# Expert weights of a mixture-of-experts layer: odd pieces issued by GpSimd, even pieces by SyncE

## The reference, cut to what matters

```
def hier_moe(h, lp):
    x = h.reshape(Bn * T, D)
    g_logits = x @ lp['router_group_w'] + lp['router_group_b']
    g_star = argmax(g_logits)                       # one group of 4 experts per token
    ...                                             # top 2 experts in the group -> gate
    hid = silu(einsum('nd,edf->nef', x, lp['expert_w1'])) * einsum('nd,edf->nef', x, lp['expert_w3'])
    y = einsum('nef,efd->nd', hid * gate[:, :, None], lp['expert_w2'])
```

## Time and profile before

| what | value |
|---|---|
| median of 3 runs | 2029.57 us (2023.04 to 2037.4) |
| the profiled execution's own time | 2022.37 us |
| its span, first to last instruction | 2020.7 us |
| start of the first item's gather / of its first matmul | 1358.15 / 1372.97 us |
| stages of the four items from the turn of one item to the next | about 157 us each, 1374 to 2003 us |
| PE, DVE, ACT, POOL busy | 81%, 60%, 40%, 14% of the span |

### The profile page before, as it was taken

How to read it: one execution, slowest core, us unless ns; L and a number is a source line. 1 busy time by engine, 2 the same in 40 slices (tenths; PEclk the granted TensorE clock), 3 DMA queues, 4 the chain that set the end, 5 groups by cost and what they waited for, 6 DMA issues and landing times. The chain is left out here.

```text
span 2020.7 us, 25909 instructions
## 1 busy us (share of the span) xinstructions
PE 1639.8 (81%) x8192; PEld 1285.0 (64%) x8192; DVE 1205.8 (60%) x1686; ACT 808.1 (40%) x997; POOL 274.9 (14%) x352
## 2 busy tenths in 40 slices
PE   4899999999789788884502489657999999999998
PEld 3799996555677555553301367555786787787785
DVE  4233323653344445545798653465788788788788
ACT  4222223434255323231100432214676676577575
POOL 1000004342200445422234000010000000000000
PEclk9899999999677799997755689858999999999999
DMA  5744459996343668752000274135998898898897
GB/s 163 218 137 132 137 136 183 163 162 99 73 161 100 140 145 181 154 111 59 0 0 3 85 208 166 44 120 179 336 374 281 324 372 300 306 360 318 296 371 257
DMA packets 325410, 371.74 MB, mean 184 GB/s; under 512 B 193845, under 2 KB 227922, under 8 KB 314850
## 3 DMA queue, kind: packets, MB, share of 16 engines
q1 hardware_dynamic: 309650, 327.71, 53.7%
q0 software_dynamic: 14544, 43.01, 9.6%
q10 hardware_dynamic: 1152, 0.26, 0.1%
HBM read 362.84 MB, written 19.47 MB: 189 GB/s over the span
## 5 line engine op out<-in xcount | busy, mean ns | idle before, releaser
L154 DVE TENSOR_TENSOR w_low<-w_raw,w_high 128x2048 fp32r<-128x2048 f32 x212 | 484.6, 2291 | 159.5 <-ACT w_high L150 158.1
L150 ACT CAST w_high<-w_raw 128x2048 fp32r<-128x2048 f32 x212 | 403.8, 1911 | 234.7 <-PE ex_A L161 126.8
L159 PE MATMUL ex_A<-w_high,ex_XT_high 128*128 128x512 f32 x512 | 209.9, 410 | 0.0
L160 PE MATMUL ex_A<-w_low,ex_XT_high 128*128 128x512 f32 x512 | 207.3, 405 | 0.0
L161 PE MATMUL ex_A<-w_high,ex_XT 128*128 128x512 f32 x512 | 207.1, 404 | 0.0
L159 PE MATMUL proj_acc<-w_in_high,hT_high 128*128 128x296 f32 x448 | 135.1, 302 | 14.9 <-DVE w_in_low L154 14.9
L446 POOL DMA_DIRECT2D cmp_pages<-in_cache_kv_cmp x128 | 87.3, 686 | 384.8 <-issue 384.8
L160 PE MATMUL proj_acc<-w_in_low,hT_high 128*128 128x296 f32 x448 | 135.2, 302 | 0.0
L161 PE MATMUL proj_acc<-w_in_high,hT_low 128*128 128x296 f32 x448 | 134.7, 301 | 0.0
L569 PE MATMUL cmp_zps<-cmp_xT,cmp_w1s 128*128 128x512 f32 (+1 forms) x288 | 119.2, 569 | 10.3 <-DVE cmp_xT L623 6.7
L154 DVE TENSOR_TENSOR w_in_low<-w_in_slot,w_in_high 128x1184 fp32r<-128x1184 f32 x56 | 76.5, 1389 | 81.0 <-ACT w_in_high L150 81.0
(11 more groups left out here) (519 smaller groups left out, 3070.0 us busy)
## 6 DMA issues: line engine op xcount, KB each, us to landing
w_raw<-in_expert_w SPq DMA_DIRECT2D x196, 1024.0 KB, 5.3
w_in_slot<-in_w_in SPq DMA_DIRECT2D x56, 592.0 KB, 5.0
cmp_pages<-in_cache_kv_cmp POOLq DMA_DIRECT2D x128, 128.0 KB, 7.9
cmp_pages<-in_cache_kv_cmp SPq DMA_DIRECT2D x128, 128.0 KB, 6.9
w_raw<-in_w_out SPq DMA_DIRECT2D x16, 1024.0 KB, 6.4
sel_k_rows<-in_cache_kv_sel POOLq DMA_DIRECT2D x64, 128.0 KB, 3.4
sel_k_rows<-in_cache_kv_sel SPq DMA_DIRECT2D x64, 128.0 KB, 3.5
sel_v_rows<-in_cache_kv_sel SPq DMA_DIRECT2D x64, 128.0 KB, 3.8
```

The costliest lines, as they stand in the source:

```text
L150: return copy(high.bitcast(F32R), x)
L154: return dve.tensor_tensor(low.bitcast(F32R), x, high, ALU.subtract)
L159: pe.matmul(out, r(a_high), r(b_high), start=start, stop=False)
L160: pe.matmul(out, r(a_high), r(b_low), start=False, stop=False)
```

## The change

Odd pieces (1, 3, 5, ...) are issued by POOL, even pieces remain with SP. The waits on `w_low` are the same ones. Before each odd piece POOL also waits for its previous pace instruction and runs a new one, a 1x1 tensor_tensor on `pace` that reads `eps` twice. POOL's loop over items now issues odd pieces 5 to 15, then the gather of the next item, then odd pieces 17 to 47, then pieces 1 and 3 of the next item. The first gather still comes ahead of the loop.

```diff
@@ phase_out @@
             stream_load(sp, z)
-            for n in range(RING):
+            for n in range(0, RING, 2):
                 sp.wait_ge(z.low, 4 * NCH - 3 + n)
                 expert_piece(sp, m, io, 0, n)
+
+        @block.gpsimd
+        def _(pool):
+            for n in range(1, RING, 2):
+                pool.wait_ge(z.low, 4 * NCH - 3 + n)
+                expert_piece(pool, m, io, 0, n)
...
 PLACES_AT = 8
+FETCH_AT = PLACES_AT + 9
@@ phase_moe @@
+        def load(eng, w, item, chunks):
+
+            e0 = eng.value_load(m.plan[0:1, bass.ds(item, 1)], min_val=0, max_val=12)
+            for n in chunks:
+                eng.wait_ge(w_low, w * CHUNKS + (n + 1))
+                if n % 2:
+                    eng.wait_ge(paced, w * (CHUNKS // 2) + ((n - RING) // 2 + 1))
+                    eng.tensor_tensor(pace[:], eps[:1], eps[:1], ALU.mult).then_inc(paced, 1)
+                expert_piece(eng, m, io, e0, n)
...
             pool.sem_inc(paused, 1)
+            pool.sem_inc(paced, 1)
...
             fetch(0)
             with pool.Fori(0, count(pool)) as w:
+                load(pool, w, w, range(RING + 1, FETCH_AT, 2))
                 pool.wait_ge(x_made, w * 4 + 4)
                 fetch(w + 1)
+                load(pool, w, w, range(FETCH_AT, CHUNKS, 2))
+                load(pool, w, w + 1, range(CHUNKS + 1, CHUNKS + RING, 2))
 
         @block.sync
         def _(sp):
             sp.sem_inc(w_low, RING)
-
-            def load(w, item, chunks):
-
-                e0 = sp.value_load(m.plan[0:1, bass.ds(item, 1)], min_val=0, max_val=12)
-                for n in chunks:
-                    sp.wait_ge(w_low, w * CHUNKS + (n + 1))
-                    expert_piece(sp, m, io, e0, n)
-
             with sp.Fori(0, count(sp)) as w:
-                load(w, w, range(RING, CHUNKS))
-                load(w, w + 1, range(CHUNKS, CHUNKS + RING))
+                load(sp, w, w, range(RING, CHUNKS, 2))
+                load(sp, w, w + 1, range(CHUNKS, CHUNKS + RING, 2))
```

More of the change, by code:

```diff
@@ L2254, in phase_moe @@
         idx = ctx.enter_context(nc.sbuf_tensor("ex_token", [P, 1], I32))
-        pause, eps = sb("ex_pause", [1, 1]), m.eps
+        pause, pace, eps = sb("ex_pause", [1, 1]), sb("ex_pace", [1, 1]), m.eps
         X = m.proj[:, 0, D:2 * D]
@@ L2267, in phase_moe @@
         id_made, id_ready, x_in, paused = n_("id_made"), n_("id_ready"), n_("x_in"), n_("paused")
+        paced = n_("paced")
         order = ORDER
```

## The result

| kernel | median | runs |
|---|---|---|
| before, on the same chip | 2026.3 us | 2021.97 to 2037.4, 4 runs |
| after | 2118.01 us | 2103.98 to 2121.63, 4 runs |

The ratio is 1.0431, 95% interval 1.0364 to 1.0498: slower by some 90 us, and above the top of the range.

The account below looks back on a forecast made before the run. PE was taken to set the pace, with the DMA engines close behind at 98% busy. All steady terms cost 0 and only the start gained: 2029.57 - 3.4 = 2026.2 us, range 2009 to 2066 us.

Parts of the forecast that it names:

- trigger and landing: Odd pieces on POOL in the steady stretch: 6.1 us from DVE's end to landed, 0.9 us to spare, cost 0.
- The 6.96 us of a turn: Part of one buffer's 11.20 us left for trigger, issue and landing after 4.24 us from ACT's start to DVE's end.
- The trigger, 0.42 us: Time from DVE's end to POOL's issue of an odd piece, read at the gather, against SP's 0.17 us.
- about three times an item: How often DVE runs two low parts back to back; only there would a pace lose 2.29 us, swallowed, cost 0.
- Rival 2: Pace waits behind DVE's low part; if every odd piece met it, +42 us, 2068 us; chance 0.08.
- 2 us of idle time in front: Sign of a slower outcome: pace instructions on POOL preceded by 2 us of idle time.
- The landing, 5.7 us: Landing of a POOL piece: SP's 5.3 us plus POOL's longer issue, 0.75 against 0.37 us.
- shares 0.4 us ... and can lose that much: Contention of two queues: a POOL piece overlaps the next SP piece by 0.4 us, within its 0.9 to spare; cost 0.
- 2.63 us per MB against 2.80: Two queues' throughput at the stage's start against steady demand of one piece per 2.80 us: fits with 6% left.
- The cushions: Steady stretch: 1.5 us to spare in SP's reload, plus 3.9 us that ACT may be late before PE waits.
- Rival 1: POOL's pieces land late and the buffers bind: PE loses 9.9 d - 3.9 four times, middle 2064 us; chance 0.16.
- The start, -3.4 us: Stage start: with fewer pieces beside it, the first gather lands at 1363.9 instead of 1367.25 us, a 3.4 us gain.

## Why the prediction was wrong

The step that failed is "trigger and landing are 0.42 + 5.7 = 6.1 of 6.96: 0.9 us to spare, PE keeps its pace, cost 0". In the medians they took 0.67 + 7.2 = 7.9 us without the pace, and with it 2.2 + 7.5 = 9.7 where the pace was long; PE stood still in the changed kernel, and a turn took 14.70 us instead of 11.20.

- **The bound** was read rightly: PE at the limit and the DMA engines close behind, more to lose than to win. The 6.96 us of a turn were right too: 14.70 - 11.20 = 3.50 us were lost in just this place.
- **The trigger, 0.42 us, failed.** It was read at the gather, behind a short DVE instruction. For a piece it is 0.69 us (low part's end at 1640.65 to the issue at 1641.34) where the pace is short. It is 2.2 us where the pace is long: the first of the two low parts ended at about 1634.66, half of 4.50 after 1632.41, and the issue came at 1636.90. So a POOL piece comes 1.0 us later than SP's even without the pace, not 0.6.
- **"So the pace is through before the next low part" and "about three times an item" failed.** Some 44% of the pace instructions met a low part, about ten an item. The count of back-to-back low parts came from a trace in which loads were spaced evenly; the change itself makes them come in pairs. Rival 2 was dismissed by that count. Its sign, "2 us of idle time in front" of the pace, came in another form: the instruction itself is recorded as 2.08 us long.
- **The landing, 5.7 us, and "shares 0.4 us ... and can lose that much" failed.** POOL's queue alone gave 6.1, so the queue's own price was nearly right. What was missing is that late odd loads lengthen all landings: 6.7 to 7.7 us on any mix of queues, SP's pieces too. "2.63 us per MB against 2.80" counts only the mean demand; in the changed kernel the pairs leave the engines idle between them (0.00 in the slices above). Why 0.7 us of lateness on SP alone lengthens a landing from 5.3 to 7.3 us is not shown.
- **The cushions did not cover it.** The 1.5 us to spare held only as long as the landing stayed at 5.3, and the 3.9 us are used up once if every turn is over: 0.7 us of lateness already cost 0.8%.
- **Rival 1's formula came near**, with other inputs. Without a pace: d = 0.73 + 7.3 - 6.96 = 1.07, 4 x (9.9 x 1.07 - 3.9) = +27 us, measured +37. With the pace ahead, trigger between 0.69 and 2.2, at 44% long about 1.4, and 7.5: d = 1.9, +60; all turns as the worst one, d = 3.5, +123; measured +92 by the medians. Rivals 1 and 2 came at once, and feed each other; the chances had them as alternatives.
- **The start, -3.4 us, was half right**: PE waited 8.4 us for 10.22, a gain of 1.8. It drowned.
- **The clock was not in the sum.** Some 24 of the 81.6 us appear as PE running slower after waits. How much of that would have been waiting otherwise was not tried.

## What to carry to other kernels

Where a ring of buffers feeds an engine with little to spare, read not only how long a load takes but how late and how evenly loads are issued: here two engines that answered the same event 1 us apart made every second load late, and all loads landed later. If an instruction only marks the time, let it not read SBUF beside a neighbour with two inputs from there, or put it behind the issue. A duration or a count taken from an even stream does not hold for the stream that the change makes, so price the change's own rhythm first.

## What was not expected of the hardware

- POOL's 1x1 tensor_tensor took up to 2.27 us when it began beside DVE's low part, which has both inputs in SBUF, and 0.18 us beside DVE instructions that read ex_B from PSUM; the 1x1 memset took 0.09 us always.
- One register read, with a semaphore increment, put SP's issue 0.7 us later; three put it 1.8 us later.
- With all pieces on POOL they landed in 6.1 us (median), at the same 359 GB/s in the steady stretch as SP's; two hardware queues together cost nothing that could be told (1.002).
- One 2.3 us stand of PE was followed, 1 us later, by three slices of 1 us at a granted clock of 0.50.
